# A hybrid decoder step on one core: another order of the small steps inside the mixer

## The reference

```python
h = rmsnorm(x, n_mix)
qg, kg, vg, rg, a_low, qs, ks, vs = split(h @ w_in)
log_a = log_sigmoid(a_low @ w_a2 + b_a) / 16
o_g, s_new = gla_chunked(qg * dk**-0.5, kg, vg, log_a, s0)    # 4 heads, chunks of 64
o_g = o_g * rsqrt(mean(o_g * o_g) + eps) * gla_g * silu(rg)   # mean per head
o_s = rmsnorm(sink_attention(rope(qs), rope(ks), vs), swa_g)  # window 128, 8 heads, 2 kv heads
x = x + concat([o_g, o_s]) @ w_out
# gla_chunked, for each chunk, b = cumsum(g):
att = where(causal, (q * exp(b)) @ (k * exp(-b)).T, 0)
o = att @ v + (q * exp(b)) @ S
S = exp(b_last) * S + (k * exp(b_last - b)).T @ v
```

## Time and profile before

| | us |
|---|---|
| median of 3 runs (lowest, highest) | 1955.02 (1954.67, 1956.83) |
| the profiled execution | 1954.67 |
| its span, first to last instruction | 1952.8 |
| PE busy | 1914.8 |
| DVE busy | 1341.2 |
| ACT busy | 1098.3 |
| POOL busy | 1094.3 |

### The profile page before, as it was taken

How to read it: one execution, slowest core, us unless ns; L and a number is a source line. 1 busy time by engine, 2 the same in 40 slices (tenths; PEclk the granted TensorE clock), 3 DMA queues, 4 the chain that set the end, 5 groups by cost and what they waited for, 6 DMA issues and landing times.

```text
span 1952.8 us, 40743 instructions
## 1 busy us (share of the span) xinstructions
PE 1914.8 (98%) x15466; PEld 1886.5 (97%) x15466; DVE 1341.2 (69%) x2492; ACT 1098.3 (56%) x2230; POOL 1094.3 (56%) x811
## 2 busy tenths in 40 slices
PE   5999999999999999999999999999999999999997
PEld 5999999998999999999999999999999999999997
DVE  7975677576464986678678757865764568857774
ACT  4664566635344665466656646664453466646662
POOL 3666566732225666566766656666313266655663
PEclk9999999999999999999999999999999999999998
DMA  3233233331213232322323332333212222332331
GB/s 139 82 108 104 93 98 103 114 106 64 90 44 111 77 103 96 105 99 95 101 83 102 105 98 93 104 95 135 78 53 90 90 82 93 95 111 90 104 109 60
DMA packets 92114, 185.65 MB, mean 95 GB/s; under 512 B 12880, under 2 KB 22768, under 8 KB 91376
## 3 DMA queue, kind: packets, MB, share of 16 engines
q1 hardware_dynamic: 84096, 170.04, 26.5%
q10 hardware_dynamic: 7824, 13.00, 1.9%
HBM read 178.09 MB, written 6.95 MB: 95 GB/s over the span
## 4 chain that ended last, share of the span: by engine, by line
PE 93%; DVE 4%; ACT 1%; issue 1%; DMA 0%; POOLq 0%; POOL 0%; DVEq 0%; ACTq 0%
PE ps L819 57%; PE ps L779 23%; PE ps L828 7%; PE ps L1051 1%; PE ps L1040 1%; PE ps L807 1%; PE ps L1201 1%; PE ps L1023 1%; PE ps L799 0%; PE ps L1062 0%; DVE g_buf L2311 0%; PE ps L1164 0%; DVE h_end L1724 0%; DMA x<-xT 0%; DVE x L2375 0%
## 5 line engine op out<-in xcount | busy, mean ns | idle before, releaser
L819 PE MATMUL ps<-rhs,w_hi 128*128 128x272 f32 x4256 | 806.0, 289 | 0.0
L819 PEld LDWEIGHTS ps<-rhs,w_hi 128*128 128x128 f32 x4256 | 669.9, 188 | 1.4 <-DVE ssum L1911 1.1
L819 PE MATMUL ps<-rhs,w_lo 128*128 128x272 f32 x2128 | 613.8, 288 | 0.0
L656 POOL TENSOR_TENSOR w_lo<-w_raw,w_hi 128x512 fp32r<-128x512 f32 x272 | 351.0, 1295 | 253.0 <-ACT w_hi L1327 252.9
L819 PEld LDWEIGHTS ps<-rhs,w_lo 128*128 128x128 f32 x2128 | 402.3, 189 | 0.0
L650 POOL TENSOR_TENSOR w_lo<-w_raw,w_hi 128x1024 fp32r<-128x1024 f32 x80 | 191.4, 2394 | 353.3 <-ACT w_hi L1271 338.8
L819 PE MATMUL ps<-act_c,w_hi 128*128 128x272 f32 x1792 | 354.4, 289 | 1.1 <-DVE h_mid L1762 0.7
L656 POOL TENSOR_TENSOR w_lo<-s_tmp,w_hi 128x512 fp32r<-128x512 f32 x216 | 282.6, 1320 | 33.0 <-ACT w_hi L1327 32.8
L819 PEld LDWEIGHTS ps<-act_c,w_hi 128*128 128x128 f32 x1792 | 287.7, 188 | 1.8 <-DVE h_mid L1762 1.2
L779 PE MATMUL ps<-h_mid,w_hi 128*128 128x272 f32 x1600 | 279.3, 293 | 0.0
L819 PE MATMUL ps<-act_c,w_lo 128*128 128x272 f32 x896 | 258.2, 288 | 0.0
(11 more groups left out here) (292 smaller groups left out, 3182.7 us busy)
## 6 DMA issues: line engine op xcount, KB each, us to landing
w_raw<-stream SPq DMA_DIRECT2D x380, 256.0 KB, 2.9
w_raw<-stream SPq DMA_DIRECT2D x80, 512.0 KB, 3.3
g_buf<-stream SPq DMA_DIRECT2D x52, 256.0 KB, 2.8
pl_raw<-stream SPq DMA_DIRECT2D x64, 192.0 KB, 2.8
x<-xT ACTq DMA_DIRECT2D x8, 272.0 KB, 5.9
y_d<-x SPq DMA_DIRECT2D x8, 272.0 KB, 2.1
s<-s_d ACTq DMA_DIRECT2D x2, 1024.0 KB, 6.7
s_s_d<-s ACTq DMA_DIRECT2D x2, 1024.0 KB, 3.9
```

The lines of the kernel that those rows point to most:

```text
L656: pool.tensor_tensor(operand(w_lo, j, half), source(op, s, half), operand(w_hi, j, half).bitcast(F32), ALU.subtract).then_inc(pool_low, 1)
L819: ins = pe.matmul(bank(s, at), w[:, k * P:(k + 1) * P], moving[:, k, side, r, :], start=fresh and k == 0 and w is hi and side == 0, stop=k ...
```

## The change

Six edits, nearly all in the table of steps:

1. "squares" comes behind rG2 in `JOBS` in place of ahead of it, and so does its chain; its steps `s_norm` and `smix` come later too.
2. In slot 17 `gs_o` and `att` 0 come ahead of `kv` 0 and 1. `att` 0 then waits for `ga_out` and `kv` 0 for `att_out`, as the other `kv` do.
3. `att` 2, `o` 1, `kv` 4 and 5 come in slot 19, which is now rG2's.
4. `gs_kv` 0 moves from behind out5 to behind squares, `klm` from behind out2 to behind `kv` 3, `gs_kv` 1 from behind out6 to behind out4, and `store` with it.
5. The waits on `gkv_used` at `gs_kv` 1 and at the first product of the second output half are dropped.
6. `gatef` becomes two steps, one for each half of the gate.

```diff
-        "vG0", "vG1", "vG2", "vG3", "rG0", "rG1", "squares", "rG2", "rG3"] + [f"out{n}" for n in range(KT)]
+        "vG0", "vG1", "vG2", "vG3", "rG0", "rG1", "rG2", "squares", "rG3"] + [f"out{n}" for n in range(KT)]
...
-            17: [("kv", 0), ("kv", 1)] + [("ssq", j) for j in range(4)] +
-                [("gs_o", 0), ("gsq", 0), ("s_add", 0), ("att", 0)],
...
+            17: [("gs_o", 0), ("gsq", 0), ("att", 0), ("kv", 0), ("kv", 1)] + [("ssq", j) for j in range(4)],
...
             # output_half
                         pe.wait_ge(m["gmix_ready"], NBLK + 1)
-                        pe.wait_ge(m["gkv_used"], 2)
...
             # kv, PE
-                        if i < 2:
-                            pe.wait_ge(m["ga_out"], 1)
-                            pe.wait_ge(m["v_out"], 5)
-                        else:
-                            pe.wait_ge(m["att_out"], i // 2 + 1)
+                        pe.wait_ge(m["att_out"], i // 2 + 1)
...
             # att, PE
-                        pe.wait_ge(m["state_made"], 2 * max(i, 1))
-                        if i:
-                            pe.wait_ge(m["att_out"], i)
+                        if i == 0:
+                            pe.wait_ge(m["ga_out"], 1)
+                        else:
+                            pe.wait_ge(m["state_made"], 2 * i)
...
             # gs_kv, PE
-                        if i:
-                            pe.wait_ge(m["gkv_used"], i)
...
             # gatef, ACT
-                        act.wait_ge(m["in_used"], JOBS.index("z1") + 1)
-                        for log, z in ((t2, t1), (t4, shuf)):
-                            link(act.activation(log[:, :], z[:, :], ACT.Abs))
-                        for log in (t2, t4):
-                            link(act.activation(log[:, :], log[:, :], ACT.Exp, scale=-1.0))
-                        for log in (t2, t4):
-                            act.activation(log[:, :], log[:, :], ACT.Ln, bias=1.0).then_inc(m["z_logged"], 1)
+                        z = (t1, shuf)[i]
+                        act.wait_ge(m["in_used"], JOBS.index(f"z{i}") + 1)
+                        log = (t2, t4)[i]
+                        link(act.activation(log[:, :], z[:, :], ACT.Abs))
+                        link(act.activation(log[:, :], log[:, :], ACT.Exp, scale=-1.0))
+                        act.activation(log[:, :], log[:, :], ACT.Ln, bias=1.0).then_inc(m["z_logged"], 1)
```

More of the change, by code:

```diff
@@ L159, in mixer_steps @@
             7: [("samp_q", 0)],
-            10: [("gatef", 0)],
+            10: [("gatef", 0), ("gatef", 1)],
             11: [("gate", 0)],
@@ L167, in mixer_steps @@
                  ("vtr", 4), ("gs_att", 0)],
-            17: [("kv", 0), ("kv", 1)] + [("ssq", j) for j in range(4)] +
-                [("gs_o", 0), ("gsq", 0), ("s_add", 0), ("att", 0)],
[L170 to L173, removed]
+            17: [("gs_o", 0), ("gsq", 0), ("att", 0), ("kv", 0), ("kv", 1)] + [("ssq", j) for j in range(4)],
+            18: [("att", 1), ("o", 0), ("kv", 2), ("kv", 3), ("klm", 0), ("o_norm", 0), ("s_add", 0)],
+            19: [("att", 2), ("o", 1), ("kv", 4), ("kv", 5), ("o_norm", 1)],
+            20: [("s_norm", 0), ("gs_kv", 0), ("smix", 0), ("smix", 1)],
+            21: [("att", 3), ("smix", 2), ("o", 2), ("kv", 6), ("kv", 7), ("smix", 3), ("o_norm", 2)] +
+                [("silu", j) for j in range(4)],
             22: [("o", 3), ("o_norm", 3), ("otr", 0), ("otr", 1), ("gmix", 0)],
             23: [("gmix", 1), ("gss", 0), ("otr", 2)],
-            24: [("gbc", 0), ("otr", 3), ("gmix", 2), ("klm", 0)],
+            24: [("gbc", 0), ("otr", 3), ("gmix", 2)],
             25: [("gmix", 3), ("gmix", 4)],
-            27: [("gs_kv", 0)],
-            28: [("gs_kv", 1)],
-            29: [("store", 0)]}
+            26: [("gs_kv", 1), ("store", 0)]}
     unit_slots = [4, 5, 6, 7, 9, 11, 12, 13, 14, 15]
```

## The result

The changed kernel takes 1969.2 us (median; 1969.1 to 1970.3), the kernel before 1955.8 beside it: ratio 1.0069, 95% interval 1.0057 to 1.0082. The profiled execution took 1969.81 us (span 1968.0), 15.1 more than that of before. The forecast, 1961.8 with a range to 1966.0, had the sign and half of the size.

A forecast was written before the change was run, and what follows sets the result against it. PE, 93% of the span, was taken to bound the kernel. Terms 0.5 + 0.4 + 1.1 + 1.3 + 0.1 = 3.4 us a mixer, 6.8 for both, on 1954.67 plus 0.35 gave 1961.8 us; range 1957.5 to 1966.

The forecast's parts named there:

- A: kv 0 behind att 0: PE idles 0.95 us for the masked copy, at half clock; costs 0.5 us a mixer.
- B: gs_kv 0 behind o 1: new wait 1.43 us for o_out 2, less 1.05 at kv 4; net 0.4 a mixer.
- D: gs_kv 1 behind out4: waits for gmix_ready 5, the last gla low parts; 1.3 us a mixer.
- C: out0 behind the later mixS chain on DVE: its third step waits 1.1 us a mixer, bounds 0 and 1.6.
- E: gatef in two steps: two more ACT table loads, 2.56 us, nearly all absorbed; 0.1 us a mixer, crumbs included.
- R1: Rival, chance 0.13: DVE slightly quicker, so waits hide each other and only gs_kv 1's wait stays; 1957.6 us.
- R2: Rival, chance 0.15: PE's clock falls again near gs_kv 0 or stays low longer behind gs_o; some 1965 us.
- R3: Rival, chance 0.06: clock stays up behind gs_o, now directly after a dense projection; up to 8.3 us back, 1953.5.

The follow-up runs named there:

- 4: Changed kernel with kv 0 and kv 1 again ahead of gs_o and att 0: median 1967.2 us, net (without the clock's share) 1953.4 against 1953.8.
- 2: Changed kernel with gs_kv, klm, store and their waits back among the output projections: median 1968.4 us, net 1948.0 against 1953.8.
- 6: Kernel before with only squares and the mix steps later: median 1962.3 us, net 1944.6 against 1940.3.
- 1: Changed kernel with gatef as one step for both tiles again: median 1968.9 us, net 1951.2 against 1953.8.
- 5: Kernel before with only gatef split in two steps: median 1955.8 us, net 1943.4 against 1940.3.
- Run 8: Kernel before with squares and mix steps later, GpSimd's subtraction beside smix 2 held until the four low parts are made: median 1956.9 us, net 1942.0.
- 9: Whole changed kernel with both GpSimd subtractions, at the gate and beside smix 2, held back: median 1963.9 us, net 1947.8 against 1953.8.
- 7: Kernel before with gatef split and GpSimd's subtraction there held until the probabilities are scaled: median 1954.9 us, ratio 1.0001, net 1940.5.
- 3: Changed kernel with GpSimd's subtraction beside smix 2 held until the four low parts are made: median 1966.2 us, net 1950.6 against 1953.8.

## Why the forecast was too small, point by point

Per mixer; the net differences of the table are halved.

| part | forecast | measured | from |
|---|---|---|---|
| A | 0.5 | 0.2 ± 0.3 | 4 |
| what gs_kv brings: new wait of B, D, addition in C | 1.9 | 2.9 ± 0.5 | 2 |
| squares later: rest of C, less kv 4's wait | 0.9 | 2.1 ± 0.4 | 6 |
| E | 0.1 | 1.3 to 1.5 | 1, 5 |

The prediction didn't split B + C + D = 2.8 in this way; its own sums do. With gs_kv away, out0's third step would be ready 2.81 + 12.4 - 1.26 = 13.95 us after kv's start, and PE there after 1.43 + 6.2 + 2.22 + 0.6 + 1.55 = 12.0: a wait of 1.95, less 1.05 at kv 4, is 0.9, and 1.9 are left. Run 8, squares later with VectorE not held, measured 0.7.

The measured parts add up to 6.5 to 6.7, twice that is 13.0 to 13.5; net, the change cost 13.1 to 13.4. In plain time it cost 13.4 against the executions of before beside it, and about 15 against the means of the 62 others, 2 of them the clock's share. With both collisions taken out (9) it cost net 7.1, 3.6 a mixer, where the forecast had 3.4.

**B and D held.** gs_kv 0 came 1.52 us behind where it could have (554.02 + 0.83 to 556.37) and was forecast at 1.43; gs_kv 1 waited 1.30, forecast 1.3. The wait at kv 4 went.

**A's wait came, its price is open.** The idle time was as forecast (0.94 for 0.95), in a stretch at half clock. Net it cost 0.2 ± 0.3 us, in plain time 1.0; the half that I took is neither confirmed nor refuted.

**C is the step that failed most.** The prediction put it: "smix 2 and low part 1.33 (557.94 to 559.27)". That price was read from a row of before that ran with GpSimd idle. In the new order smix 2 follows the end of rG3, as GpSimd's subtraction does, and the pair takes 3.3 us. In the row of before no subtraction of GpSimd ran between 557.13 and 563.28. The bound of 1.6 was made from DVE's rows alone, so it could not hold it; measured 3.44. Take the collision away and out0 is 1.50 longer, with a wait of 1.01, forecast 1.1: the chain itself was nearly right.

**E is the same mistake.** The prediction weighed 2.56 us of loads against a head start of 1.14 and 1.42 us "to spare" in front of the Exp. The loads are 1.28 us with no drain, as said, and ACT's balance came out (7), but what ends the Exp's wait is DVE, and on ACT behind the gate stands w_hi, which releases GpSimd, which holds DVE. Of the three engines I followed one. The 1.42 us in the earlier trace rows had 0.7 us of this hold in it already (0.88 for 0.17 us of work), a sign that could have been seen. The upper bound, 1.1, was close to the 1.3 to 1.5 by luck: it stood for a missing head start.

**R1** (waits hide each other) did not happen. **R2** (the clock falls once more, or the stretch behind gs_o gets longer) came in part: the new fall is seen behind out0 in runs 2 and 6 and not in the changed kernel's profile, but the stretch of its second mixer is longer, and the clock's share of its time is 15.7 us in the mean against 13.1 to 13.6 before. **R3** was wrong for this change: with gs_o directly behind a dense product the clock still fell (windows of the changed kernel, same two places; before 0.51 and 0.83):

```profile
528.00:538.00 10.00, 9.06 (x69) 8.41 (x69) 2.15 (x6) 2.83 (x7) 5.86 (x3) 0.66 0.16 54
1487.00:1507.00 20.00, 19.05 (x135) 18.22 (x134) 3.44 (x7) 3.89 (x8) 6.13 (x3) 0.74 0.09 28
```

Its price, up to 8.3 us, was not reached: in the three kernels that keep the clock up at both places the clock's share fell by 4 to 6 us.

**Open.** In the changed kernel's profile one matmul behind the first mixer, in the second feed-forward half of layer 0, waited 0.7 us for a copy of ACT; runs 5 and 6 have it too, 1 to 4 and 7 to 9 do not. Its cause wasn't tried. Nor was why the half-clock stretch lasts longer in some executions than in others, what A costs with the clock counted in, and why out0 is 1.50 longer where C's sum had 1.1.

## What to carry over

Before moving a VectorE operation with two SBUF inputs, lay GpSimd's row beside VectorE's: if both hang on the end of one product, they will meet each time (here in both mixers of each kernel without the hold), and the price of even a 4-column addition is what is left of GpSimd's instruction. A GpSimd result that is needed much later can be held until the meeting is over; no new wait of PE came of it here, and it gave back net 3.2 us for the one and 2.9 for the other. Compare medians only after looking at the granted clock: a part that costs 2.6 us was hidden by it. But look at the time too: an edit that gained 5.8 us net gained 0.8 in all, since behind its two longer stops the clock fell to half.

## What the runs showed of the hardware

- A 128x4 VectorE addition of 0.17 us took 2.19, a 128x544 product of 0.78 took 2.76, a 128x544 subtraction of 0.72 took 2.91, each begun under a GpSimd subtraction of 2.4 us. A reduction with one SBUF input (1.22) and a masked copy from PSUM (0.78, begun before the subtraction) kept their times. With the subtraction held back the addition took 0.17 and the product 0.78.
- In or right behind a row of 32 matmuls of 8 columns the clock fell to half, for 7 to 10 us in both mixers before and in the changed kernel, for as little as 3.4 in run 6; with the same 32 in groups of six or four between dense matmuls it stayed at 1.00, in both mixers of the three profiled executions.
- Two waits of 1.57 us with 1.0 us of matmuls between them were followed by half clock in four mixers of four; waits of 1.10 and about 1.57 us at the same place were not, in six of six.
- A table load of ACT took 1.28 us, and the next ACTIVATE started 0.01 to 0.02 us behind it.
